# VectorE's weight splits, gates and first decays at other beats, and a last-pass gather through two banks, in a one-core hybrid decoder layer

## The reference

```python
mod = (c_act @ ada_w[l] + ada_b[l])[:, None, :]
h = rmsnorm(x, norm_mix[l]) * (1.0 + sc_mix) + sh_mix
proj = h @ w_in
...
y_gla = gla_mixer(gla_q, gla_k, gla_v, gla_r, gla_glr, ...)   # 4 heads
y_ml = mlstm_mixer(ml_q, ml_k, ml_v, ml_o, ml_i, ml_f, ...)   # 4 heads
y_gdn = gdn_mixer(gdn_qkv, gdn_z, gdn_a, gdn_b, ...)          # 8 heads
gates = jax.nn.sigmoid(merge.astype(jnp.float32)).reshape(b, s, N_BRANCHES, D_MODEL)
y = gates[:, :, 0] * y_gla + gates[:, :, 1] * y_ml + gates[:, :, 2] * y_gdn
x = x + gt_mix * (y @ w_out)
h = rmsnorm(x, norm_ffn[l]) * (1.0 + sc_ffn) + sh_ffn
x = x + gt_ffn * swiglu(h, w_ffn_up[l], w_ffn_down[l])
return rmsnorm(x, norm_final)
```

## Time and profile before

| | |
|---|---|
| median of three runs | 2761.28 us |
| lowest, highest | 2759.69, 6485.82 us |
| the profiled execution, as a whole | 2759.64 us |
| its span | 2757.7 us |
| granted TensorE clock over the span | 0.987 |
| busy: TensorE, VectorE, ScalarE, GpSimd | 95%, 69%, 36%, 18% |

### The profile page before, as it was taken

One profiled execution on the slowest core, in us unless ns is written; L12 is line 12 of the kernel. 1 busy time (PEld: TensorE's weight loads), 2 busy tenths in 40 slices (PEclk: granted clock), 3 DMA queues, 4 the chain that ended last, 5 costly groups with the idle time before them and its releaser, 6 DMA issues.

```text
span 2757.7 us, 44502 instructions
## 1 busy us (share of the span) xinstructions
PE 2633.1 (95%) x16384; PEld 2312.8 (84%) x16384; DVE 1900.8 (69%) x3625; ACT 997.1 (36%) x2236; POOL 497.2 (18%) x433
## 2 busy tenths in 40 slices
PE   7999999999999999999999999998999999999998
PEld 3789789889888978988998897897878888888887
DVE  4677777867867777766775775776576666666656
ACT  4633653563374365344336326333430000000002
POOL 0000410310130040000000000000044433333440
PEclk9999999999999999999998998999999999999999
DMA  6221131122022112113212212323021111111111
GB/s 205 54 81 32 43 75 47 31 81 57 14 61 81 28 43 77 45 39 79 51 32 66 62 32 50 87 70 117 25 77 47 54 53 47 46 46 46 46 47 61
DMA packets 225176, 160.87 MB, mean 58 GB/s; under 512 B 28240, under 2 KB 207544, under 8 KB 224960
## 3 DMA queue, kind: packets, MB, share of 16 engines
q1 hardware_dynamic: 212288, 150.15, 18.4%
q0 software_dynamic: 12672, 7.87, 2.9%
...
## 4 chain that ended last, share of the span: by engine, by line
PE 69%; DVE 20%; ACT 9%; issue 2%; DMA 0%; SPq 0%; DVEq 0%; ACTq 0%
PE bank L179 27%; PE bank L171 16%; PE bank L2111 8%; DVE sig L1052 3%; PE bank L972 2%; PE bank L1227 2%; PE bank L1219 2%; DVE wB_lo L1105 1%; DVE wA_lo L1105 1%; PE bank L448 1%; PE bank L1176 1%; DVE feat_region L1661 1%; DVE feat_region L1375 1%; PE bank L1549 1%; DVE sig L1050 1%
## 5 line engine op out<-in xcount | busy, mean ns | idle before, releaser
L171 PE MATMUL bank<-wB_hi,h_hi 128*128 128x256 f32 x1024 | 299.7, 293 | 4.2 <-ACT feat_region L1009 2.7
L171 PE MATMUL bank<-wA_hi,h_hi 128*128 128x256 f32 x1024 | 297.7, 291 | 4.2 <-ACT feat_region L1009 2.7
L171 PE MATMUL bank<-wB_lo,h_hi 128*128 128x256 f32 x1024 | 299.9, 293 | 0.0
L171 PE MATMUL bank<-wB_hi,h_lo 128*128 128x256 f32 x1024 | 299.5, 292 | 0.0
L171 PE MATMUL bank<-wA_hi,h_lo 128*128 128x256 f32 x1024 | 297.5, 291 | 0.0
L171 PE MATMUL bank<-wA_lo,h_hi 128*128 128x256 f32 x1024 | 297.5, 291 | 0.0
L179 PE MATMUL bank<-h_hi,wA_hi 128*128 128x512 f32 x672 | 267.3, 398 | 2.7 <-DVE feat_region L985 2.2
L179 PE MATMUL bank<-h_hi,wB_lo 128*128 128x512 f32 x672 | 267.5, 398 | 0.0
L179 PE MATMUL bank<-h_hi,wB_hi 128*128 128x512 f32 x672 | 267.3, 398 | 0.0
L179 PE MATMUL bank<-h_hi,wA_lo 128*128 128x512 f32 x672 | 267.2, 398 | 0.0
L179 PE MATMUL bank<-h_lo,wA_hi 128*128 128x512 f32 x672 | 266.4, 396 | 0.0
...
## 6 DMA issues: line engine op xcount, KB each, us to landing
w_raw<-in_w_in_dram SPq DMA_DIRECT2D x96, 512.0 KB, 3.6
w_raw<-in_w_ffn_up_dram SPq DMA_DIRECT2D x44, 512.0 KB, 3.8
...
w_raw<-in_w_ffn_down_dram SPq DMA_DIRECT2D x22, 512.0 KB, 3.4
conv_in<-row_scratch SPq DMA_DIRECT2D x16, 512.0 KB, 4.3
rows_region<-in_x_dram SPq DMA_DIRECT2D x8, 512.0 KB, 7.8
...
```

Of the source, the lines that this page charges most:

```text
L171: mm = nc.tensor.matmul(bank[:, n_out:n_out + n1 - n0], (h_hi, h_lo)[hp][:, k, t * P:t * P + P], buf[wp][:, k, n0:n1], start=(s == 0), sto ...
```

## The change

Both kernels have the same arithmetic. What moves:

- **Splits.** Each kind of group gets its own beats for its two high and four low parts (the table SPLIT, beats from b0), and a half is loaded in the beat of its last low part.
- **z gates.** ZG_AT has other beats for the eight gate computations of the GDN output.
- **Gates.** The transpose and what follows stand one beat later, and `gates_dve` stands ahead of the chunk's work in VectorE's beat.
- **First decays.** The preparation of GLA chunks 0 and 1 is 17 and 2 beats earlier (`prep_at`), so that those of chunk 0 stand in beats 51 and 52 of the first half and those of chunk 1 in 71 and 72, where 68, 69, 73 and 74 were. The two halves of kt_sub change places.
- **Tail.** The units of the first two output groups come in another order, the transposes of tiles 5 to 7 in beats 2 to 9 (2, 4, 5, 6, 7, 9), part q = 1 of tiles 0 to 3 in bank M[1], and SP issues the loads of x ahead of its wait for the transposes of tile 6.

```diff
@@ -882,7 +882,8 @@
     for j in range(4):
         groups.append(([out_v[:, :, m * P:(m + 1) * P] for m in (2 * j, 2 * j + 1)], P))
     first = len(units)
-    units.extend((OUT0 + j, "out", t, N_IT - 1, j) for j in range(2) for t in range(NT))
+    for j, ts in ((0, range(5)), (1, range(2)), (0, range(5, NT)), (1, range(2, NT))):
+        units.extend((OUT0 + j, "out", t, N_IT - 1, j) for t in ts)
     AHEAD = 3
...
...
@@ -1128,13 +1129,13 @@
...
     def rows_pe(pe, i, r):
-        if r == GATES_AT[i] + 2:
+        if r == GATES_AT[i] + 3:
             pe.wait_ge(sem("gate_pre"), i + 2)
             nc.tensor.transpose(M[5][0:2 * NT, 256:256 + P], gq[:, 0:2].rearrange("p q t -> p (q t)"), ident[:]) \
...
...
@@ -1743,27 +1744,38 @@
             step(tt(g_row[:, :, 0], gex[:, 0], gh[:, 1], ALU.add))
             step(tt(gex[:, 1], gh[:, 3], gq[:, 2], ALU.add))
             step(dve.tensor_copy(gex[:, 2], gh[:, 3]), "gate_pre")
-        if r == GATES_AT[i] + 3:
+        if r == GATES_AT[i] + 4:
             dve.wait_ge(sem("gate_e"), h + 1)
             step(stt(gq[:, 3], gex[:, 0], -1.0, gh[:, 2], ALU.mult, ALU.mult))
     after = {g: unit_done[u] + 1 for g, u in last_unit.items()}
-    split_at = {}
+
+
+    SPLIT = {"v": ((0, 2), (3, 7, 11, 12)), "rg0": ((0, 2), (6, 10, 14, 16)), "rg1": ((0, 2), (2, 3, 8, 9)),
+             "gqk": ((0, 2), (3, 7, 8, 17)), "gv": ((0, 2), (4, 5, 9, 10)), "zg": ((0, 3), (5, 5, 6, 7)),
+             "qk": ((5, 7), (6, 7, 11, 12))}
+    split_at, lo_at, load_at = {}, {}, {}
     for g in range(len(groups)):
         b0 = after[g - 2] if g >= 2 else 8 * g
-        split_at.setdefault(b0, []).append((g, 0))
-        split_at.setdefault(b0 + (2 if g < OUT0 else 1), []).append((g, 1))
-    load_at = {}
-    for b, gs in split_at.items():
-        for g, h in gs:
+        _, kind, _, i, r = units[first_unit[g]]
+        if g >= OUT0:
+            his, los = (0, 1), (1, 2, 2, 3)
+        elif i < 0 or kind == "qk" and i == 0:
+            his, los = (0, 2), (1, 2, 3, 4)
+        else:
+            his, los = SPLIT[f"rg{r}" if kind == "rg" else kind]
+        for h in range(2):
+            split_at.setdefault(b0 + his[h], []).append((g, h))
+            for part in range(2):
+                lo_at.setdefault(b0 + los[2 * h + part], []).append((g, h, part))
             if g + 1 < len(groups):
-                load_at.setdefault(b + 2, []).append((g + 1, h))
+                load_at.setdefault(b0 + los[2 * h + 1], []).append((g + 1, h))
     units_at = {}
     for u, b in unit_done.items():
         units_at.setdefault(b, []).append(u)
-    ZG_AT = [2 + 4 * t for t in range(NT)]
+    ZG_AT = [0, 3, 7, 12, 18, 22, 26, 30]
     def place(b):
...
@@ -1773,6 +1785,15 @@
         if i == N_IT:
             i, r = N_IT - 1, r + B1 + B2
         return (i, r, None) if r < B1 else (i, None, r - B1)
+
+    def prep_at(b, offset):
+
+        for early in range(2):
+            at_ = chunk_at(b + EARLY_PREP[early], offset)
+            if at_ and at_[1] == early and branch(at_[0]) == "gla":
+                return at_
+        at_ = chunk_at(b, offset)
+        return at_ if at_ and at_[1] >= 2 and branch(at_[0]) == "gla" else None
     def chunk_at(b, offset):
...
@@ -1805,9 +1826,14 @@
     GT_AT = {}
     for t in range(NT):
         u = next(u for u in range(N_UNITS) if units[u][1:] == ("rg", t, N_IT - 1, 1))
-        b = max(unit_done[u] + 1, max(GT_AT.values(), default=0) + 1, 0 if t < GT_INNER else P2_LAST + 2)
-        GT_AT.update({(t, 0): b, (t, 1): b + 1})
-    assert GT_AT[GT_INNER - 1, 1] < P2_LAST - 4
+        b = max(unit_done[u] + 1, max(GT_AT.values(), default=0) + 1)
+        GT_AT.update({(t, 0): b, (t, 1): b + 1} if t < GT_INNER else
+                     {(t, q): P2_LAST + ((2, 4), (5, 6), (7, 9))[t - GT_INNER][q] for q in range(2)})
+
+    def gt_bank(t, q):
+
+        return M[1] if q and t < GT_INNER - 1 else M[5]
+    assert GT_AT[GT_INNER - 1, 1] < P2_LAST - 4 and GT_AT[GT_INNER - 2, 1] + 2 < P2_LAST - 5
     O2_DONE = [unit_done[unit_of("o2", t)] for t in range(NT)]
...
...
@@ -1865,11 +1891,13 @@
             for t in (0, 1, 2, 3, 5, 6, 7):
                 x_load(sp, t, 0, 256)
         if r == 4:
+            sp.wait_ge(sem("sig_used"), N_GATES)
+            x_load(sp, 4, 0, 256)
+            for t in range(4):
+                x_load(sp, t, 256, D)
             sp.wait_ge(sem("gt_up"), 2 * 6)
-            sp.wait_ge(sem("sig_used"), N_GATES)
             gt_load(sp, 7)
-            x_load(sp, 4, 0, 256)
-            for t in range(NT):
+            for t in range(4, NT):
                 x_load(sp, t, 256, D)
             for t in (6, 7):
                 part_load(sp, t)
...
@@ -1882,17 +1910,17 @@
...
                     pe.wait_ge(sem("gdn_y"), NT * N_IT - (2 if t < GT_INNER else 0))
-                    if n:
-                        pe.wait_ge(sem("gt_lo"), n)
+                    before = [m for m in range(n) if gt_bank(*divmod(m, 2)) is gt_bank(t, q)]
+                    if before:
+                        pe.wait_ge(sem("gt_lo"), before[-1] + 1)
                     for j, k in enumerate(range(4 * q, min(4 * q + 4, EARLY_K))):
-                        tp = nc.tensor.transpose(M[5][:, j * P:j * P + P], gt_src(t, k), ident[:])
+                        tp = nc.tensor.transpose(gt_bank(t, q)[:, j * P:j * P + P], gt_src(t, k), ident[:])
...
...
@@ -2173,6 +2201,7 @@
     PREP_DVE, PREP_ACT, PREP_POOL, SCORES, OUTPUT = -8, -7, -5, 1, 4
+    EARLY_PREP = (17, 2)
     ML_PREP_PE, ML_PREP_DVE, ML_PREP_ACT = -5, (-4, -2), -3
     with nc.Block() as block:
...
@@ -2328,20 +2357,21 @@
...
                     gdn_out_dve(dve, step, i, NT - 1)
+                if r2 is not None and i < N_IT - 1:
+                    gates_dve(dve, step, i, r2)
                 for offset, stage in ((SCORES, 0), (OUTPUT, 1), (OUTPUT + 2, 2)):
                     at_ = chunk_at(b, offset)
                     if at_:
                         chunk_dve(dve, step, *at_, stage)
                 for stage in range(2):
-                    at_ = chunk_at(b, PREP_DVE + stage)
-                    if at_ and branch(at_[0]) == "gla":
+                    at_ = prep_at(b, PREP_DVE + stage)
+                    if at_:
                         prep_dve(dve, step, *at_, stage)
                 for stage in range(2):
                     at_ = chunk_at(b, ML_PREP_DVE[stage])
                     if at_ and branch(at_[0]) == "ml":
                         ml_prep_dve(dve, step, *at_, stage)
                 if r2 is not None and i < N_IT - 1:
-                    gates_dve(dve, step, i, r2)
...
...
@@ -2357,9 +2387,8 @@
...
                         split_gate(dve, step, g, h)
-                for part in (1, 0):
-                    for g, h in split_at.get(b - 1 - part, ()):
-                        split_lo(dve, step, g, h, part)
+                for g, h, part in lo_at.get(b, ()):
...
```

More of the change, by code:

```diff
@@ L1493, in prep_pool @@
             n = 64 * (half + 1)
[L1494 removed]
+            sub = kt_sub[:, 1 - c % 2, 4 * half:4 * half + 4, 0:n]
             pool.wait_ge(sem("gla_ek"), 2 * C + half + 1)
@@ L1817, in _build @@
     assert len(NORM_AT) == 7 and max(NORM_AT) < BEATS and NRM_AT[-1] + 2 < BEATS
[L1818 to L1820 removed]
+    YT_AT = {P2_LAST + max(CHUNK2 * t + 8, 11): t for t in range(NT)}
+    assert all(b0 <= next(b for b in range(BEATS) for v, s0, s1 in fill[b]
+                                if v == unit_of("out", t, 2) and s1 > 18) for b0, t in YT_AT.items())
     H0 = 2 * KT
```

44 lines of the change are left out of this document (20 added, 24 removed).

## The result

| | before | changed |
|---|---|---|
| median of four runs | 2761.3 us | 2695.15 us |
| runs of the changed kernel | | 2699.73, 2699.51, 2690.79, 2690.48 us |
| span of the profiled execution | 2757.7 us | 2697.6 us |
| granted clock over the span | 0.987 | 0.988 |

The account below looks back on a forecast made before the run. TensorE, busy 95% of the span, was taken as the bound, with only its idle time and halved clock to win, mostly from late VectorE. Terms of 62.9 us off 2759.6, plus 1.7 for the median, gave 2698 us, range 2664 to 2736.

Parts of the forecast that it names:

- Gates (-13.6): Gate instructions a beat later, ahead of the chunk's work: all 13.6 us of L1133's waits go, bounds 10 to 13.6.
- zg low halves (-4.7): Second halves: L1564 and L1009 waits shrink or go, a new wait before the first zg matmul costs 12.9 us; net 4.7.
- Clock (-17): Three mLSTM second halves: the granted clock no longer drops behind stalls, 17 us won, bounds 0 and 19.7.
- rival C: Halved clock stays or moves: new zg wait acts with the old one, solver's GLA wait passes 2.5 us; 2727 us, chance 0.15.
- Solver (-8): First halves: rg0 and gqk low halves leave the solver's beats, early decays cost 5.2 us in GLA passes; net 8 us.
- decays (-5.6): GLA passes, beat 71: decays leaving beats 68, 69, 73 and 74 remove L1243's 5.6 us, bounds 3 to 7.
- z gates (0): ZG_AT's gate computations, the same instructions up to 6 beats earlier, taken at nothing.
- qk (-3): Second half: qk low halves leave beats 27 to 30 for 32 to 38, L1016's 3.0 us go, bounds 1 to 4.
- Gather (-11): Last pass's gather: 11 of 14.4 us of L1888's waits and missing clock go, bounds 3 and 14.
- rival B: More room than seen: zg low halves ready in time and first decays fit beats 51 and 52; 2672 us, chance 0.17.
- E: Slower by over 2%: weights come too late, as each next half loads after the last low half; chance 0.04.

Follow-up runs that it names:

- the better version: The changed kernel with two of the four zg low parts moved to b0+1 and b0+2 and GLA chunk 1's decays one beat earlier: 2680.36 us, ratio 0.9702.

## Why the prediction came out, step by step

The sum came out, 60.1 us in the spans against 62.9, and in part that is luck. The clock was won back in the mLSTM passes and lost in the GLA passes, near to nothing in all where 17 us were forecast; first halves and GLA second halves gained more than their terms and covered it.

1. **Gates (-13.6):** right. Alone 10 to 19 us, L1133 gone, nothing new.
2. **zg low halves (-4.7):** in the GLA passes the waits came nearly as worked out, in the mLSTM passes the new one did not. L1564 and the L1009 wait fell as said, the new wait of the zg matmul is 2.2 us in GLA passes (forecast 1.8), and 0.6 us in one mLSTM pass alone (forecast 1.9 in three), so 9.3 us against 12.9, and by the waits the term is 7.9 us.
3. **Clock (-17):** this is the step that failed. In the mLSTM passes it came: their second halves are 29.0 us shorter, where the terms put there (9.0 gates, 17 clock, 1 for the qk parts, and nothing net for zg) give 27. By the windows the missing clock there went from 19.7 us to (0.02 x 80) + (0.02 x 81) = 3.2. But "the clock as kept" was extended from one row, 1.65 us at 1.00, to a stall of 1.8 us, and the GLA passes had one of 2.2. It lost (0.06 x 91) x 2 + (0.04 x 89) x 2 = 18 us there, as much as the mLSTM passes won. It is rival C's mechanism and the wait that C named, but C priced it in the mLSTM halves, and for the GLA passes it named the solver's wait. Without this loss the GLA second halves would be some 17 us shorter than before, where the terms for them (4 gates, 4.7 zg, 1.3 qk) give 10; what gave the rest isn't shown. The profiled execution would then have been near 2682 us (an estimate), which is where the runs with moved low parts are.
4. **Solver (-8), decays (-5.6):** the first halves of passes 0 to 6 gave 21.7 us, 8 more than these two terms. rg0 and gqk give some 10 us of first halves each with the rest in place. The decays' net was right and its parts were not: 5.2 lost against 5.6 gained was forecast, no difference was measured. By the waits, the loss is 10.4 us, 4.4 at L1239, 1.2 at L1228 and 4.8 in ScalarE's queue in beat 73, which the forecast did not have; against it stand L1244's 5.6 and the 4.9 of L179 that the early decays avoid, which it did not have either.
5. **z gates (0):** wrong as a cost at nothing. Back at their old beats they cost 10.6 us of first halves, and only 2.3 us of that is in the listed waits of L1220 (5.4 in place of 3.1). The moves were not independent of each other.
6. **qk (-3):** right, L1017 waits 0.2 us.
7. **Gather (-11):** too large. 7 us by the run without it. L1917 waits 4.0 us, just at the bound given, and L973 now waits 3.0 us for the sums of L986 in place of 1.9 for L985.

Of rival B, the first half (the zg low parts ready in time) is what the better version makes nearly true, with 0.6 us left of the wait; the decays did not fit for nothing. E did not show: no wait of TensorE is for a load of weights, and ScalarE waits once for w_raw, 2.2 us, as it did before (2.3).

Which executions keep the clock is partly chance: the four runs are two at 2699.6 with clocks of 0.988 and 0.987 and two at 2690.6 with 0.991. That the wait for the zg parts sets the fall off is shown: it goes with the wait gone (old beats, or two parts moved), and comes with it in 22 of 24 cases. That the length of the wait alone does it is not shown. Why 1.5 us halves it in two passes and not in the other two stays open, and the rival that the thin matmuls just ahead (L1716, 1.84 us) have a share in it stands untested, since no run left them out; the falls behind 0.53 us and the same thin matmuls speak for it.
